# Two-layer decoder trunk: another order of the last down products at each stage end, and a weight split moved from unit 21 to unit 20

## The chip, the cores and the metric

One core of one Trainium2 chip runs the whole trunk in one launch. The metric is the device time of one execution in microseconds (us), the median of several runs.

## What is computed

x is 256 tokens by 1024 channels in float32. The trunk has two layers; each is a sandwich of feed-forward (FFN), mixer, FFN, and each of the six steps ends in a layer norm of the scaled residual:

```python
for i in range(DEPTH):
    x = post_norm(x, 0.5 * swiglu(x, w_gate[i, 0], w_up[i, 0], w_down[i, 0]), ln_g[i, 0], ln_b[i, 0])
    mix = pool_mixer(x, ...) if i % 2 == 0 else swa_sink_attention(x, ...)
    x = post_norm(x, mix, ln_g[i, 1], ln_b[i, 1])
    x = post_norm(x, 0.5 * swiglu(x, w_gate[i, 1], w_up[i, 1], w_down[i, 1]), ln_g[i, 2], ln_b[i, 2])
```

swiglu is silu(x Wg) * (x Wu), times Wd, with 2816 hidden channels. Layer 0 mixes by trailing means over 2, 4, 8 and 16 tokens and a linear map for each group of channels; layer 1 by windowed attention with 16 query heads, 4 key and value heads and sinks.

## The kernel before, in words

**Arithmetic.** Products run in a 32-bit matmul type on values that are split in two: `hi` is the value rounded to that type (a ScalarE copy), `lo` what is left (a VectorE subtraction). A product of two such values is three matmuls. Every weight is loaded raw by the SP queue, split by ScalarE (ACT, `*_hi`) and VectorE (DVE, `*_lo`), and some halves of the low part by GpSimd (POOL, `low_half`). `g_split` does a gate and up unit in two halves, `d_split` a down unit.

**Stages.** There are four FFN stages, f = 0 to 3, of 22 units of 128 hidden channels. For a unit, TensorE (PE) makes gate and up for all 256 tokens (`gate_up`), ACT and DVE make silu(gate) * up and its two parts, and PE multiplies by the down weights (`ffn_down`), adding into four PSUM banks ACC[t][h]: t is the token half (128 tokens), h the column half (512 of 1024 channels). One call for one t and one h is a group of three matmuls of 128x512 (lines 1226 to 1228, called by `down`); the last unit counts `acc_done` for each bank. Down of a unit runs a unit or more behind its gate and up.

**Stage end.** `last_u` is 18. Behind the gate and up of unit 21 PE issues, in this order: unit 19, t=0, h=1; unit 18, t=1, both h; units 20 and 21 of t=0, first h=0, then h=1; units 19 to 21 of t=1, first h=0, then h=1. The DVE norm (`layer_norm`, lines 942 to 973) takes t=0 and then t=1, each column half as its bank is counted: sum with the residual (L942), statistics (L948), centring (L960) and scaling (L973), with POOL's power for 1/sqrt. PE transposes the normed token half by column halves (`transposes`, L1328, four for each), ACT and DVE split it (L630, L989), and the next stage's first two units are done by token halves (`gate_up_tokens`, L1261 to L1266). Between stage 0 and stage 1 stands the pool mixer (`pool_pe`: `means` at L1043, `maps` at L1057); between stages 2 and 3 attention (`attention_pe`), whose output product `wo` uses the same `down`, k = 0 to 7, with k 5 to 7 of t=1 last by column halves.

**Order on the queues.** All order is written out by hand; each engine runs its instructions in program order, with waits on counting semaphores. `g_used` counts units whose gate and up are complete, so that their weight slots may be written; `d_used` the same for down slots; `g_hi_done`, `g_lo_done`, `h_hi_done`, `h_lo_done` count the parts. The first two units of the next stage are split at this stage's end: unit 0 at unit 20, and unit 1 at unit 21, where ACT does both halves of `hi` (line 599 and following), DVE the first half of `lo` (line 903 and following) and POOL the second. G0 is the number of units before a stage. The wait ahead of ACT's copies is

```python
if f is None:      # attention's q, k and v weights, behind stage 2
    after(act, g_used, G_QKV + (-1, 0, 0, 1, 3, 4)[u])
...
else:
    after(act, g_used, G0[f] + (-1, 0, 0, 2)[u] if u < 4 else G - 1 + 4 * it)
```

and the silu of a unit in `DIRECT` (0, 1 and 21) waits for `g_used >= G0[f] + u + 1`.

Of the kernel before, what the change touches and what calls it, by code (L numbers as in the profile page):

```python
# [27 lines left out]
UNITS = F // P  # L28
# [7 lines left out]
WINDOWS = (2, 4, 8, 16)  # L36
GC = D // len(WINDOWS)
# [7 lines left out]
POOL_UNITS = 2  # L45
# [24 lines left out]
def trunk_kernel(nc, x, positions, ln_g, ln_b, w_gate, w_up, w_down, pool_w, pool_b, pool_scale,  # L70
# [8 lines left out]
    with ExitStack() as ctx:  # L79
# [137 lines left out]
        def pool_raw(j):  # L217
            return raw_d[:, (D_POOL // 2) % 2, j, :]
# [30 lines left out]
        def next_first(f, u):  # L249
            return (f + 1 if f != 2 else None, u)  # L250
# [286 lines left out]
        def _(act):  # L537
# [42 lines left out]
            def unit(f, u, it=0):  # L580

                ahead = next_splits(f, u, it)
                if u not in DIRECT:
                    low_of(f, u, it)
                    for a in ahead[0:1]:
                        g_split(*a, halves=(0,))
                    silu_of(f, u, it)
                    for a in ahead[0:1]:
                        g_split(*a, halves=(1,))
                else:  # L590
                    silu_of(f, u, it)
                    for a in ahead[0:1]:
                        g_split(*a)
                h_hi_of(f, u, it)
                if f == 0 and u == 0:
                    g_split(0, RAW_UNITS)
                if u + 1 < UNITS:
                    d_split(D0[f] + u + 1, it)
                if f == 0 and u == UNITS - 2:
                    g_split(1, 0)  # L600
                if f < 3 and u == UNITS - 1:
                    g_split(*next_first(f, 1))

            def silu_tokens(f, t):
                act.wait_ge(*((tokens_done, f) if t == 0 else (g_used, G0[f] + 2)))
# [237 lines left out]
        def _(dve):  # L843
# [38 lines left out]
            def unit(f, u, it=0):  # L882

                ahead = next_splits(f, u, it)
                if u not in DIRECT:
                    gate_up_sum(f, u, it)
                    for a in ahead[0:1]:
                        g_split(*a, halves=(0,))
                    h_of(f, u, it)
                    for a in ahead[0:1]:  # L890
                        g_split(*a, halves=(1,))
                else:
                    h_of(f, u, it)
                    for a in ahead[0:1]:
                        g_split(*a)
                h_lo_of(f, u, it)
                if f == 0 and u == 0:
                    g_split(0, RAW_UNITS)
                if u + 1 < UNITS:
                    d_split(D0[f] + u + 1, it)  # L900
                if f == 0 and u == UNITS - 2:
                    g_split(1, 0, halves=(0,))
                if u == UNITS - 1:
                    if f == 0:
                        g_split(1, 0, halves=(1,))
                    elif f < 3:
                        g_split(*next_first(f, 1), halves=(0,))

            def h_tokens(f, t):
                dve.wait_ge(silu_done, UNITS * f + t + 1)  # L910
# [121 lines left out]
                else:  # L1032
                    layer_norm(5)

        def pool_pe(pe):

            def means(t, src, columns, first, last):

                for k in range(KT):
                    if k % 4 == 0 and t == src:  # L1040
                        pe.wait_ge(xn_done, 2 * t + k // 4 + 1)
                    out_ = ps[:, WORK + 2 * t + k // 4, (k % 4) * P:(k % 4 + 1) * P]
                    ins = pe.matmul(out_, xn[:, src, k * P:(k + 1) * P], band[:, k // 2, columns:columns + P],  # L1043
                                    start=first and k % 4 == 0, stop=last and k % 4 == 3)
                    if t == 0 and k == 0:
                        ins.then_inc(d_used, 1)
                    elif last and k % 4 == 3:
                        ins.then_inc(u_done, 1)

            def maps(t):  # L1050
                if t == 0:
                    pe.wait_ge(d_scaled, POOL_UNITS)
                for g in range(len(WINDOWS)):
                    if g % 2 == 0:
                        pe.wait_ge(u_sb, 2 * t + g // 2 + 1)
                    for j in range(2):
                        ins = pe.matmul(ACC[t][g // 2][:, (g % 2) * GC:(g % 2 + 1) * GC], uT[t][:, 2 * g + j, :],  # L1057
                                        pool_raw(j)[:, g * GC:(g + 1) * GC], start=j == 0, stop=j == 1)
                    if g % 2 == 1:
                        ins.then_inc(acc_done, 1)  # L1060

            pe.wait_ge(band_in, 16)
            pe.wait_ge(hf_done, UNITS)
            means(0, 0, 0, True, True)
            means(1, 0, P, True, False)
            maps(0)
            means(1, 1, S, False, True)
            maps(1)

        def attention_pe(pe, three, down, transposes):  # L1070

            ident = cst[:, 0, :]
            e = QKV_EVENT
# [91 lines left out]
                down(D_WO + k, xT_hi[:, k, :], xT_lo[:, k, :], ts, k == 0, k == WO_UNITS - 1, hs=hs)  # L1165

            transposes(e, 0)
            qkv(0, 0, 0, part=0, d_counted=True)
            qkv(0, 1, 0, part=0)
            qkv(0, 0, 0, part=1)  # L1170
# [43 lines left out]
                for k in (6, 7):  # L1214
                    wo(k, (0,), hs=(h,))
            for h in range(2):
                for k in range(5, 8):
                    wo(k, (1,), hs=(h,))


# [1 line left out]
        def _(pe):  # L1222
# [28 lines left out]
            def gate_up_tokens(f, t):  # L1251
# [6 lines left out]
                for k in range(KT):  # L1258
                    if k % 4 == 0:
                        pe.wait_ge(x_hi_done, 4 * e + 2 * t + k // 4 + 1)  # L1260
                    pe.matmul(out_, xT_hi[:, k, tok], w_hi[:, :, :, k, :], start=k == 0, stop=False)  # L1261
                    pe.matmul(out_, xT_hi[:, k, tok], w_lo[:, :, :, k, :], start=False, stop=False)  # L1262
                for k in range(KT):
                    if k % 4 == 0:
# [49 lines left out]
            def ffn_down(f, u, ts=(0, 1), it=0, hs=(0, 1)):  # L1314
# [5 lines left out]
                final = u == UNITS - 1  # L1320
                down(E, hT_hi[:, E % D_SLOTS, :], hT_lo[:, E % D_SLOTS, :], ts, u == 0, final, it, hs)

            def transposes(e, t, used=0):

                for q in range(2):
                    pe.wait_ge(*((xn_done, 4 * e + 2 * t + q + 1) if e > 0 else (x_in[t], 16)))
                    for k in range(4 * q, 4 * q + 4):
                        last = pe.transpose(x_bank(e, t, q)[:, (k % 4) * P:(k % 4 + 1) * P], xn[:, t, k * P:(k + 1) * P], ident)  # L1328
                        if k == 0 and used:
                            last.then_inc(d_used, used)  # L1330
                    last.then_inc(tr_done, 1)

            pe.wait_ge(ident_in, 16)
            for f in range(FFNS):
                e = FFN_EVENT[f]

                transposes(e, 0, used=(0, 2, 1, 1)[f])
                if f == 0:
                    gate_up_raw(0)
                    transposes(e, 1)  # L1340
# [24 lines left out]
                ffn_down(f, last_u + 1, (0,), hs=(0,))  # L1365
                gate_up(f, last_u + 3)
                ffn_down(f, last_u + 1, (0,), hs=(1,))
                ffn_down(f, last_u, (1,))
                for h in range(2):
                    for u in (last_u + 2, last_u + 3):  # L1370
                        ffn_down(f, u, (0,), hs=(h,))
                for h in range(2):
                    for u in range(last_u + 1, UNITS):
                        ffn_down(f, u, (1,), hs=(h,))
                if f == 0:
                    pool_pe(pe)
                if f == 2:
                    attention_pe(pe, three, down, transposes)

# [1 line left out]
_INS = ["x", "positions", "ln_g", "ln_b", "ffn_w_gate", "ffn_w_up", "ffn_w_down", "pool_w", "pool_b", "pool_scale",  # L1381
# [36 lines left out]
```

## Time and profile before

| | |
|---|---|
| median of 3 runs | 860.23 us (860.13 to 860.37) |
| profiled execution, its time | 860.7 us |
| its span | 858.9 us |
| PE busy | 841.1 us, 98% |
| DVE busy | 562.8 us, 66% |
| ACT busy | 419.3 us, 49% |
| POOL busy | 45.8 us, 5% |
| mean granted TensorE clock | 0.997 |

The span is the time from the first to the last instruction in the trace; the execution's own time has 1.8 us around it. The starts of matmuls are observed, their ends are modelled: a matmul of 128x512 is shown with some 0.4 us, but the next starts 0.23 us later, so neighbours overlap. Idle time in brackets is that of the engine just before the instruction, with what ended it.

### The profile page before, as it was taken

What the parts mean: (1) busy time and instruction counts of PE and PEld (TensorE: products, weight loads), DVE (VectorE), ACT (ScalarE), POOL (GpSimd) and SP (SyncE); (2) the same over time, 40 slices, a digit from 0 to 9 for tenths busy, and PEclk for the clock granted to TensorE, in tenths of its full rate; (3) what the DMA queues carried; (4) which work ended last, traced back from release to release, by engine and by line L of the source; (5) the groups of instructions that cost most, each with busy time, mean ns of one, the idle gap of its engine ahead of it and who ended that gap; (6) DMA issues with size and microseconds to landing.
All of it is one profiled execution on the core that took longest, in us unless ns stands there. A gap on an engine that the chain in (4) does not pass through costs nothing.

```text
span 858.9 us, 12145 instructions
## 1 busy us (share of the span) xinstructions
PE 841.1 (98%) x4484; PEld 711.5 (83%) x4484; DVE 562.8 (66%) x777; ACT 419.3 (49%) x651; POOL 45.8 (5%) x59
## 2 busy tenths in 40 slices
PE   7999999999999999999999999999999999999995
PEld 6888888888888888887888888887766888888885
DVE  2785655669846565668665565669898855655656
ACT  2554454552535455454445454554665544454540
POOL 0060000013000000002000000011001000000000
PEclk9999999999999999999999999999999999999998
DMA  9997555392755655556656556553454565465501
GB/s 277 348 325 243 177 195 178 116 294 101 250 192 180 203 188 195 172 179 228 205 158 229 168 177 206 185 196 123 167 167 154 172 224 196 154 229 168 182 1 49
DMA packets 116142, 162.17 MB, mean 189 GB/s; under 512 B 3936, under 2 KB 97632, under 8 KB 116112
## 3 DMA queue, kind: packets, MB, share of 16 engines
q1 hardware_dynamic: 112656, 152.06, 53.1%
q0 software_dynamic: 2496, 9.44, 3.3%
q8 instruction: 19, 0.31, 0.1%
q10 hardware_dynamic: 960, 0.27, 0.1%
q14 instruction: 11, 0.09, 0.0%
HBM read 160.70 MB, written 1.05 MB: 188 GB/s over the span
## 4 chain that ended last, share of the span: by engine, by line
PE 91%; DVE 4%; SPq 1%; DMA 1%; ACT 1%; issue 1%; POOL 0%; DVEq 0%; ACTq 0%
PE ps L1295 29%; PE ps L1293 17%; PE ps L1226 10%; PE ps L1227 10%; PE ps L1228 10%; PE ps L1292 4%; PE ps L1261 1%; DMA raw_g<-in_ffn_w_up 1%; PE ps L1262 1%; PE ps L1266 1%; PE ps L1092 1%; PE ps L1095 1%; PE ps L1101 1%; SPq L322 1%; PE ps L1328 1%; PE ps L1057 1%
## 5 line engine op out<-in xcount | busy, mean ns | idle before, releaser
L1295 PE MATMUL ps<-xT,g_hi 128*128 128x512 f32 x1064 | 379.3, 396 | 0.0
L1293 PE MATMUL ps<-xT,g_lo 128*128 128x256 f32 x1216 | 314.2, 279 | 0.0
L1293 PEld LDWEIGHTS ps<-xT,g_lo 128*128 128x128 f32 x1216 | 229.2, 188 | 12.5
L860 DVE TENSOR_TENSOR g_lo<-raw_g,g_hi 128x1024 fp32r<-128x1024 f32 x179 | 220.4, 1235 | 24.9 <-ACT g_hi L551 24.9
L1295 PEld LDWEIGHTS ps<-xT,g_hi 128*128 128x128 f32 x1064 | 199.7, 188 | 41.2
L870 DVE TENSOR_TENSOR gu<-ps,gu 128x512 f32<-128x512 f32 x76 | 52.5, 691 | 221.9 <-ACT gu L574 221.9
L551 ACT ACTIVATE g_hi<-raw_g 128x1024 fp32r<-128x1024 f32 x184 | 192.1, 1052 | 5.2 <-DMA raw_g<-in_ffn_w_up 3.6
L574 ACT ACTIVATE gu<-ps 128x512 f32<-128x512 f32 x76 | 45.6, 600 | 273.5 <-PE ps L1295 273.5
L1226 PE MATMUL ps<-d_hi,hT_hi 128*128 128x512 f32 x352 | 137.5, 391 | 0.0
L1227 PE MATMUL ps<-d_lo,hT_hi 128*128 128x512 f32 x352 | 137.0, 389 | 0.0
L1228 PE MATMUL ps<-d_hi,hT_lo 128*128 128x512 f32 x352 | 137.0, 389 | 0.0
L864 DVE TENSOR_TENSOR d_lo<-raw_d,d_hi 128x1024 fp32r<-128x1024 f32 x96 | 117.3, 1224 | 5.9 <-ACT d_hi L559 5.8
L559 ACT ACTIVATE d_hi<-raw_d 128x1024 fp32r<-128x1024 f32 x96 | 99.8, 1046 | 4.7 <-DMA raw_d<-in_ffn_w_down 4.7
L1228 PEld LDWEIGHTS ps<-d_hi,hT_lo 128*128 128x128 f32 x352 | 66.1, 188 | 14.2
L1227 PEld LDWEIGHTS ps<-d_lo,hT_hi 128*128 128x128 f32 x352 | 66.1, 188 | 14.0
L1226 PEld LDWEIGHTS ps<-d_hi,hT_hi 128*128 128x128 f32 x352 | 66.1, 188 | 10.6
L1292 PE MATMUL ps<-xT,g_hi 128*128 128x512 f32 x152 | 60.4, 397 | 1.0 <-DVE g_lo L860 1.0
L578 ACT ACTIVATE hT_hi<-hf_sink 128x256 fp32r<-128x256 f32 x82 | 34.3, 418 | 34.5 <-DVE hf_sink L875 34.2
L880 DVE TENSOR_TENSOR hT_lo<-hf_sink,hT_hi 128x256 fp32r<-128x256 f32 x82 | 34.4, 420 | 3.4 <-ACT hT_hi L578 3.4
L875 DVE TENSOR_TENSOR hf_sink<-gu 128x256 f32<-128x256 f32 x76 | 33.3, 438 | 1.0 <-ACT gu L568 1.0
L568 ACT ACTIVATE gu<-gu 128x256 f32<-128x256 f32 x76 | 30.9, 407 | 3.2 <-DVE gu L870 3.2
L1292 PEld LDWEIGHTS ps<-xT,g_hi 128*128 128x128 f32 x152 | 28.5, 188 | 4.3 <-DVE g_lo L860 1.5
(155 smaller groups left out, 662.0 us busy)
## 6 DMA issues: line engine op xcount, KB each, us to landing
raw_d<-in_ffn_w_down SPq DMA_DIRECT2D x87, 512.0 KB, 4.0
raw_g<-in_ffn_w_gate SPq DMA_DIRECT2D x43, 1024.0 KB, 5.5
raw_g<-in_ffn_w_up SPq DMA_DIRECT2D x43, 1024.0 KB, 7.9
raw_g<-in_attn_w_qkv SPq DMA_DIRECT2D x6, 1024.0 KB, 6.3
raw_d<-in_attn_w_o SPq DMA_DIRECT2D x8, 512.0 KB, 3.8
gb<-in_ln_g POOLq DMA_DIRECT2D x5, 512.0 KB, 3.9
gb<-in_ln_b POOLq DMA_DIRECT2D x4, 512.0 KB, 5.8
xn<-in_x SPq DMA_DIRECT2D x2, 512.0 KB, 6.1
```

The lines of the kernel that those rows point to most:

```text
L551: act.activation(g_half(g_hi, g_slot(f, u), half), src(G, half), ACT.Copy).then_inc(g_hi_done, 1)
L559: act.activation(d_hi[:, E % D_SLOTS, :], raw_d[:, (E // 2) % 2, E % 2, :], ACT.Copy).then_inc(d_hi_done, 1)
L574: act.activation(gu[:, u % 2, :, :], both[:, :, S:2 * S], ACT.Copy).then_inc(low_done, 1)
L860: dve.tensor_tensor(g_half(g_lo, g_slot(f, u), half), src(G, half), g_half(g_hi, g_slot(f, u), half).bitcast(f32), ALU.subtract).then_inc( ...
L864: dve.tensor_tensor(d_lo[:, E % D_SLOTS, :], raw_d[:, (E // 2) % 2, E % 2, :], d_hi[:, E % D_SLOTS, :].bitcast(f32), ALU.subtract).then_in ...
L870: dve.tensor_tensor(gu[:, u % 2, :, :], both[:, :, 0:S], gu[:, u % 2, :, :], ALU.add).then_inc(gu_done, 1)
L1226: pe.matmul(out_, l_hi, r_hi, start=start, stop=False)
L1227: pe.matmul(out_, l_hi, r_lo, start=False, stop=False)
L1228: return pe.matmul(out_, l_lo, r_hi, start=False, stop=stop)
L1292: pe.matmul(bank, w_hi, xT[:, k, :, :], start=True, stop=False)
L1293: last = pe.matmul(bank[:, S:2 * S], w_lo, xT_hi[:, k, :], start=False, stop=False)
L1295: last = pe.matmul(bank, w_hi, xT[:, k, :, :], start=False, stop=k == KT - 1)
```

## The change

Five edits, all in the order of work:

- At a stage's end the down products of t=0 come first (units 20 and 21, each with h=0 and h=1), and those of t=1 follow by columns: units 18 to 21 of h=0, then 18 to 20 of h=1.
- The very last group (unit 21, t=1, h=1) is `last_down`. In stage 0 it is issued behind the first `means` of the pool mixer, in stages 1 and 2 behind the transposes of t=0, in stage 3 at the end, where it was.
- In attention the group k=7, t=1, h=1 of `wo` stands behind the transposes of t=0 of stage 3.
- In the pool mixer the last of the four `maps` of t=1 stands behind the transposes of t=0 of stage 1.
- In stages 1 and 2 the first half of the next stage's unit 1 is split behind unit 20 (ACT and DVE); the second half on ACT stays behind unit 21.

The `d_used` increments move with the products; no instruction is added or removed.

```diff
--- before.py
+++ after.py
@@ -598,8 +598,10 @@
                     d_split(D0[f] + u + 1, it)
                 if f == 0 and u == UNITS - 2:
                     g_split(1, 0)
+                if f in (1, 2) and u == UNITS - 2:
+                    g_split(*next_first(f, 1), halves=(0,))
                 if f < 3 and u == UNITS - 1:
-                    g_split(*next_first(f, 1))
+                    g_split(*next_first(f, 1), halves=(0, 1)[f > 0:])
 
             def silu_tokens(f, t):
                 act.wait_ge(*((tokens_done, f) if t == 0 else (g_used, G0[f] + 2)))
@@ -900,11 +902,10 @@
                     d_split(D0[f] + u + 1, it)
                 if f == 0 and u == UNITS - 2:
                     g_split(1, 0, halves=(0,))
-                if u == UNITS - 1:
-                    if f == 0:
-                        g_split(1, 0, halves=(1,))
-                    elif f < 3:
-                        g_split(*next_first(f, 1), halves=(0,))
+                if f == 0 and u == UNITS - 1:
+                    g_split(1, 0, halves=(1,))
+                elif f in (1, 2) and u == UNITS - 2:
+                    g_split(*next_first(f, 1), halves=(0,))
 
             def h_tokens(f, t):
                 dve.wait_ge(silu_done, UNITS * f + t + 1)
@@ -1032,7 +1033,20 @@
                 else:
                     layer_norm(5)
 
-        def pool_pe(pe):
+        def pool_maps(pe, t, groups):
+
+            if t == 0:
+                pe.wait_ge(d_scaled, POOL_UNITS)
+            for g in groups:
+                if g % 2 == 0:
+                    pe.wait_ge(u_sb, 2 * t + g // 2 + 1)
+                for j in range(2):
+                    ins = pe.matmul(ACC[t][g // 2][:, (g % 2) * GC:(g % 2 + 1) * GC], uT[t][:, 2 * g + j, :],
+                                    pool_raw(j)[:, g * GC:(g + 1) * GC], start=j == 0, stop=j == 1)
+                if g % 2 == 1:
+                    ins.then_inc(acc_done, 1)
+
+        def pool_pe(pe, last_down):
 
             def means(t, src, columns, first, last):
 
@@ -1042,32 +1056,21 @@
                     out_ = ps[:, WORK + 2 * t + k // 4, (k % 4) * P:(k % 4 + 1) * P]
                     ins = pe.matmul(out_, xn[:, src, k * P:(k + 1) * P], band[:, k // 2, columns:columns + P],
                                     start=first and k % 4 == 0, stop=last and k % 4 == 3)
-                    if t == 0 and k == 0:
+                    if t == 1 and src == 0 and k == 0:
                         ins.then_inc(d_used, 1)
                     elif last and k % 4 == 3:
                         ins.then_inc(u_done, 1)
 
-            def maps(t):
-                if t == 0:
-                    pe.wait_ge(d_scaled, POOL_UNITS)
-                for g in range(len(WINDOWS)):
-                    if g % 2 == 0:
-                        pe.wait_ge(u_sb, 2 * t + g // 2 + 1)
-                    for j in range(2):
-                        ins = pe.matmul(ACC[t][g // 2][:, (g % 2) * GC:(g % 2 + 1) * GC], uT[t][:, 2 * g + j, :],
-                                        pool_raw(j)[:, g * GC:(g + 1) * GC], start=j == 0, stop=j == 1)
-                    if g % 2 == 1:
-                        ins.then_inc(acc_done, 1)
-
             pe.wait_ge(band_in, 16)
             pe.wait_ge(hf_done, UNITS)
             means(0, 0, 0, True, True)
+            last_down(0)
             means(1, 0, P, True, False)
-            maps(0)
+            pool_maps(pe, 0, range(4))
             means(1, 1, S, False, True)
-            maps(1)
-
-        def attention_pe(pe, three, down, transposes):
+            pool_maps(pe, 1, range(3))
+
+        def attention_pe(pe, three, down, transposes, last_down):
 
             ident = cst[:, 0, :]
             e = QKV_EVENT
@@ -1165,6 +1168,7 @@
                 down(D_WO + k, xT_hi[:, k, :], xT_lo[:, k, :], ts, k == 0, k == WO_UNITS - 1, hs=hs)
 
             transposes(e, 0)
+            last_down(2)
             qkv(0, 0, 0, part=0, d_counted=True)
             qkv(0, 1, 0, part=0)
             qkv(0, 0, 0, part=1)
@@ -1214,7 +1218,7 @@
                 for k in (6, 7):
                     wo(k, (0,), hs=(h,))
             for h in range(2):
-                for k in range(5, 8):
+                for k in range(5, 8 - h):
                     wo(k, (1,), hs=(h,))
 
 
@@ -1258,7 +1262,9 @@
                 for k in range(KT):
                     if k % 4 == 0:
                         pe.wait_ge(x_hi_done, 4 * e + 2 * t + k // 4 + 1)
-                    pe.matmul(out_, xT_hi[:, k, tok], w_hi[:, :, :, k, :], start=k == 0, stop=False)
+                    ins = pe.matmul(out_, xT_hi[:, k, tok], w_hi[:, :, :, k, :], start=k == 0, stop=False)
+                    if f > 1 and t == 0 and k == 0:
+                        ins.then_inc(d_used, 1)
                     pe.matmul(out_, xT_hi[:, k, tok], w_lo[:, :, :, k, :], start=False, stop=False)
                 for k in range(KT):
                     if k % 4 == 0:
@@ -1320,6 +1326,9 @@
                 final = u == UNITS - 1
                 down(E, hT_hi[:, E % D_SLOTS, :], hT_lo[:, E % D_SLOTS, :], ts, u == 0, final, it, hs)
 
+            def last_down(f):
+                ffn_down(f, UNITS - 1, (1,), hs=(1,))
+
             def transposes(e, t, used=0):
 
                 for q in range(2):
@@ -1334,7 +1343,13 @@
             for f in range(FFNS):
                 e = FFN_EVENT[f]
 
-                transposes(e, 0, used=(0, 2, 1, 1)[f])
+                transposes(e, 0, used=(0, 2, 0, 0)[f])
+                if f == 1:
+                    pool_maps(pe, 1, (3,))
+                elif f == 2:
+                    last_down(1)
+                elif f == 3:
+                    down(D_WO + 7, xT_hi[:, 7, :], xT_lo[:, 7, :], (1,), False, True, hs=(1,))
                 if f == 0:
                     gate_up_raw(0)
                     transposes(e, 1)
@@ -1365,17 +1380,18 @@
                 ffn_down(f, last_u + 1, (0,), hs=(0,))
                 gate_up(f, last_u + 3)
                 ffn_down(f, last_u + 1, (0,), hs=(1,))
-                ffn_down(f, last_u, (1,))
-                for h in range(2):
-                    for u in (last_u + 2, last_u + 3):
+                for u in (last_u + 2, last_u + 3):
+                    for h in range(2):
                         ffn_down(f, u, (0,), hs=(h,))
                 for h in range(2):
-                    for u in range(last_u + 1, UNITS):
+                    for u in range(last_u, UNITS - h):
                         ffn_down(f, u, (1,), hs=(h,))
                 if f == 0:
-                    pool_pe(pe)
+                    pool_pe(pe, last_down)
                 if f == 2:
-                    attention_pe(pe, three, down, transposes)
+                    attention_pe(pe, three, down, transposes, last_down)
+                if f == 3:
+                    last_down(f)
 
 # ---- launch: one core; inputs and outputs as the reference has them ----
 _INS = ["x", "positions", "ln_g", "ln_b", "ffn_w_gate", "ffn_w_up", "ffn_w_down", "pool_w", "pool_b", "pool_scale",
```

## Rows read from the trace of the kernel before

**Rows 1.** The page: span, and shares of the chain by engine

```profile
span 858.9 us, 12145 instructions
...
PE 91%; DVE 4%; SPq 1%; DMA 1%; ACT 1%; issue 1%; POOL 0%; DVEq 0%; ACTq 0%
```

**Rows 2.** Timeline, PE, end of second FFN: start us, us, engine, line, op, idle

```profile
387.38 0.40 PE L1226 MATMUL ps<-d_hi,hT_hi 128*128 128x512 f32 x1
...
390.58 0.39 PE L1228 MATMUL ps<-d_hi,hT_lo 128*128 128x512 f32 x1
...
396.02 0.39 PE L1228 MATMUL ps<-d_hi,hT_lo 128*128 128x512 f32 x1
396.26 1.32 PE L1328 MATMUL ps<-cst,xn 128*128 128x128 f32 x8
397.69 0.47 PE L1261 MATMUL ps<-g_hi,xT 128*128 128x512 f32 x1
398.00 0.39 PE L1262 MATMUL ps<-g_lo,xT 128*128 128x512 f32 x1
```

**Rows 3.** Timeline, ACT, the same end

```profile
387.57 0.38 ACT L568 ACTIVATE gu<-ps 128x256 f32<-128x256 f32 x1 [1.90 <-PE ps L1228]
388.45 0.42 ACT L578 ACTIVATE hT_hi<-hf_sink 128x256 fp32r<-128x256 f32 x1 [0.49 <-DVE hf_sink L875]
388.77 1.99 ACT L551 ACTIVATE g_hi<-raw_g 128x1024 fp32r<-128x1024 f32 x2
396.95 1.26 ACT L630 ACTIVATE xT<-ps 128x512 fp32r<-128x512 f32 x2 [6.19 <-PE ps L1328]
```

**Rows 4.** Timeline, DVE, the same end

```profile
387.99 0.42 DVE L875 TENSOR_TENSOR hf_sink<-gu,ps 128x256 f32<-128x256 f32 x1 [1.06 <-ACT gu L568]
388.90 0.42 DVE L880 TENSOR_TENSOR hT_lo<-hf_sink,hT_hi 128x256 fp32r<-128x256 f32 x1 [0.48 <-ACT hT_hi L578]
389.85 1.23 DVE L860 TENSOR_TENSOR g_lo<-raw_g,g_hi 128x1024 fp32r<-128x1024 f32 x1 [0.53 <-ACT g_hi L551]
391.00 0.69 DVE L942 SCALAR_TENSOR_TENSOR xn<-ps,xn 128x512 f32<-128x512 f32 x1
...
395.45 1.41 DVE L973 SCALAR_TENSOR_TENSOR xn<-xn,rstd,gb 128x512 f32<-128x512 f32 x2
396.78 0.69 DVE L942 SCALAR_TENSOR_TENSOR xn<-ps,xn 128x512 f32<-128x512 f32 x1
...
398.11 0.67 DVE L942 SCALAR_TENSOR_TENSOR xn<-ps,xn 128x512 f32<-128x512 f32 x1
```

**Rows 5.** Timeline, POOL, the same end

```profile
391.23 2.39 POOL L384 TENSOR_TENSOR g_lo<-raw_g,g_hi 128x1024 fp32r<-128x1024 f32 x1 [173.77 <-DVE g_lo L860]
```

**Rows 6.** Timeline, ACT, end of third FFN

```profile
573.75 0.38 ACT L568 ACTIVATE gu<-ps 128x256 f32<-128x256 f32 x1 [1.90 <-PE ps L1228]
```

**Rows 7.** Timeline, PE, first FFN's pool mixer into the second FFN

```profile
211.47 0.47 PE L1261 MATMUL ps<-g_hi,xT 128*128 128x512 f32 x1 [0.34 <-ACT xT L630]
```

**Rows 8.** Timeline, DVE, the same boundary

```profile
208.25 1.41 DVE L973 SCALAR_TENSOR_TENSOR xn<-xn,rstd,kx 128x512 f32<-128x512 f32 x2
```

**Rows 9.** Timeline, PE, end of attention

```profile
663.28 0.39 PE L1228 MATMUL ps<-d_hi,xT 128*128 128x512 f32 x1
663.78 1.32 PE L1328 MATMUL ps<-cst,xn 128*128 128x128 f32 x8
```

**Rows 10.** Timeline, DVE, end of attention

```profile
657.45 1.22 DVE L860 TENSOR_TENSOR g_lo<-raw_g,g_hi 128x1024 fp32r<-128x1024 f32 x1
658.58 0.68 DVE L942 SCALAR_TENSOR_TENSOR xn<-ps,xn 128x512 f32<-128x512 f32 x1
```

**Rows 11.** Timeline, DVE, end of kernel

```profile
844.82 0.69 DVE L942 SCALAR_TENSOR_TENSOR xn<-ps,xn 128x512 f32<-128x512 f32 x1 [1.68 <-PE ps L1228]
```

**Rows 12.** Timeline, PE, early stall of the first FFN

```profile
28.27 0.50 PE L1292 MATMUL ps<-xT,g_hi 128*128 128x512 f32 x1 [1.04 <-DVE g_lo L860]
```

**Rows 13.** Busy time in windows, stretch behind the last matmul: PE, PEld, DVE, ACT, POOL, clock, DMA

```profile
852.00:854.00 2.00, 0.00 (x0) 0.00 (x0) 1.90 (x6) 0.00 (x0) 0.17 (x1) 0.85 0.15 54
```

## The prediction

> **What bounds the kernel.** I read the chain of waits first: 91% of it is matrix work [rows 1], so only what makes TensorE (PE) stand still, or what follows its last product, can be won or lost. The change touches six such places: five where PE turns from one set of down products to a layer norm's result, and the end. Matmul ends are modelled, so I measure PE by starts. At the end of the second FFN the 39 down products start from 387.38 to 396.02, 0.227 us apart [rows 2]; a group of three (one unit, one token half, one column half) is 0.68. The transposes follow at once, because the norm of token half 0 has just delivered [rows 2, 4]. Its first column half ends at 396.20, its second at 396.86 (the two L973 take 1.41 from 395.45, 0.75 each with an overlap). So the second four transposes start at 396.9 and are through at about 397.4; the next product starts at 397.69 and its successor 0.31 later, not 0.23. That is 0.3 of gap plus 0.1 of restart which three independent products could fill.
>
> **A group less before the norm.** The new order finishes token half 0 one group sooner: behind the last gate and up product come four groups (unit 19's, unit 20's two, unit 21's first) instead of five before the norm's first column half is summed. At the kernel's end nothing is queued on DVE in between (it waited 1.68 us for PE) [rows 11], and all that follows is DVE's chain: **-0.68**. Unit 21's values are in time there: on the second FFN's times they are ready at 388.90 + 0.42 = 389.32 [rows 4], and three groups from 387.38 end at 389.44.
>
> **The split moved to unit 20, second and third FFN.** This is the largest term. ACT's `g_split` of the next stage's unit 1 waits (lines 545 and 549, the entry 0 for unit 1) for `g_used` to reach G0 of the next stage, which is the count that gate and up of unit 21 gives. Where it stands now, behind unit 21, that is long true. Behind unit 20 it is false until PE has ended unit 21, and ACT works in order: the silu of unit 21, which waits for the same count, is queued behind the copy. The row shows ACT idle 1.90 and released by PE at 387.57 [rows 3], the same in the third FFN at 573.75 [rows 6]. So the copy runs in that silu's place, not in the idle time.
> - ACT: copy from 387.57; it takes about 1.04 (the two from 388.77 take 1.99, and DVE starts on the first at 389.85) [rows 3, 4]; the silu follows at about 388.52.
> - DVE: its subtraction of that half is also put ahead of unit 21's product. It starts at 388.65; the next instruction comes 1.15 later (389.85 to 391.00) [rows 4], so the product that stood at 387.99 stands at 389.80, 1.81 later. The rounding and the rest keep their distances: unit 21 is ready at 389.32 + 1.81 = 391.13.
> - PE: unit 21 is wanted at 389.44, so PE stalls 1.7. The products of token half 1 are queued behind it. Restart as in [rows 2]: 0.1.
> - Norm of token half 0: DVE started it 0.42 after the third product's start (390.58, 391.00) [rows 2, 4]. Now the third product starts at about 391.73, the norm at 392.16: 1.16 later, though nothing else is queued ahead of it. First half ready at 397.36, second at 398.02.
> - PE's first group behind the stall ends at 391.95, and eight more (the other column half of unit 21, seven of token half 1) end at 397.4. So it meets the norm again, transposes from 397.4 and 398.07 to 398.5, then the three products with one restart (0.76). The successor of the first gate and up product starts at 399.5 instead of 398.00 [rows 2]: **+1.5** for each of the two ends.
> - ACT's copies of the transposes (released 0.7 after their start, 396.95) [rows 3] end before 399 and aren't late. POOL's subtraction of the other half, 2.39 [rows 5], waits for ACT's second copy, which moves from 389.7 to 390.6; it ends near 394.1, ahead of its next job and of its readers at 399. No transfer changes its issue order; the loads that wait for these splits have a whole stage before them.
> - Token half 1: DVE turns to it 1.16 later (396.78) [rows 4] and reads the last accumulator 1.33 after that (398.11) [rows 4], so at 399.27. The last product now ends behind the transposes, about 399.4. That is 0.15, less than the 0.35 by which PE has moved more than DVE.
>
> **End of attention.** DVE is the one that is late: its norm starts directly behind its own subtraction (657.45, 658.58) [rows 10], not on PE. PE's last product starts at 663.28 and the transposes wait until 663.78 [rows 9]. Taking one group away ahead of them only lengthens that idle time from 0.27 to 0.95; the group costs 0.76 behind the transposes, and fills the 0.4 that [rows 2] show there. **+0.35**.
>
> **Pool mixer.** The transposes are followed by an idle 0.34 and a restart [rows 7], and four mixer products (0.9) are moved into it. But the down group behind the first pooling products makes the norm of token half 1 wait, and the transposes then wait for DVE, whose second half ended at 209.66 [rows 8] and now comes some 0.35 later. Bounds: nothing lost to PE would be -0.4, all of DVE's delay kept would be +0.1; I take **-0.1**, near the DVE side because DVE has no gap in that stretch. Moved semaphore increments cost nothing: the slots that they release are wanted a unit or more later.
>
> **Sum.** -0.68 + 2 x 1.5 + 0.35 - 0.1 = +2.6 us. The profiled execution took 860.7 (span 858.9 and 1.8 around it) and would be 863.3; the median of the runs shown is 860.23, so **862.8**.
>
> **A rule beside a row.** When PE was last idle for good, the granted clock fell: between 852 and 854, with no product in it, it was 0.85 of 2.4 GHz, on its way to 1.2 [rows 13]. The longest stall behind a product that I cite, 1.04 in the first FFN, left the next one at 0.50 [rows 12], near the 0.47 of a restart behind the short gap and far from twice the 0.40 of a product [rows 2]; the new stalls are 1.7. I take no loss of clock. The Trainium skill ("TensorE: Matmul & The Clock Gate", Part 1) says that half rate is the default state and activity releases it, so that idleness gives it back; by that rule the two new stalls would each be a chance of a slow stretch. The trace agrees that idleness lowers the clock; that a stall of this length does, no row shows.
>
> **Rivals.**
> - *The wait is no wait* (0.1, the not-slower side). If the count were reached before ACT comes to the copy, ACT would do it in its 1.90 of idle [rows 3], DVE in its 1.06 [rows 4], and unit 21 would keep 389.32. The norm would start 0.68 earlier, PE would reach the transposes 0.68 earlier with it, and the three products would fill 0.4 and be out of the way of the norm: -0.4 per end. Sum -0.68 - 0.8 + 0.35 - 0.1 = -1.2, 859.0. It decides at whether that wait is passed before 387.5. Against it: the entry in the table is 0 and the silu's own count is the same number.
> - *Part of the delay is absorbed* (0.15). The stall is there, but half of it, if ACT's copy or DVE's subtraction overlaps more than their starts show, or attention's own waits swallow the third FFN's share. Third FFN's +1.5 gone or both halved: +1.1, 861.3.
> - *The last product holds up the second norm* (0.12). The accumulator of token half 1 comes behind the transposes; if DVE then delivers late to the next transposes, some 0.3 (a gap as that at 663.5 [rows 9]) is added at each of four boundaries: +3.8, 864.0.
> - *Clock falls after the stalls* (0.03). At 1.2 GHz the eight groups of 5.5 us behind each stall would take as much again: +11 and more, 874.
> - Forecast (0.6): 862.8.
>
> **Range and chances.** The bounds of the forecast's own terms (pool mixer -0.4 to +0.1, attention end 0 to +0.4, each FFN end 1.2 to 1.7) give 861.9 to 863.4. Down to 861.2 takes in the absorbed case, up to 864.2 the held second norm; outside are the no-wait case and the clock. A measurement here tells 0.2%, 1.7 us: below 858.5 is faster, above 861.95 slower. Faster 0.04, same 0.18 (no wait, absorbed, the low edge), slower 0.78.
>
> **What would show it.** In the changed kernel's trace: ACT's copy of 128x1024 directly at the end of unit 21's gate and up, with the silu behind it; a gap of 1.7 in PE before unit 21's first down product, in the second and third FFN and not in the first and fourth; DVE's norm at the kernel's end one group sooner after the last gate and up; three products between the transposes and the next gate and up; a longer gap ahead of the transposes at attention's end. I am wrong if the silu of unit 21 starts at its old distance from PE's last product, if PE's stall there is under 1, or if the time comes out below 860.2.

## The result, and the profile after

The changed kernel takes 862.91 us (median of 7 runs, 862.23 to 863.32) beside 860.23 for the kernel before (7 runs, 859.54 to 860.57). The ratio is 1.0031, with a 95% interval of 1.0020 to 1.0042: slower by some 0.3%. The forecast was 862.8, in a range of 861.2 to 864.2.

The page of the changed kernel, span and shares of the chain:

```profile
span 861.3 us, 12145 instructions
...
PE 92%; DVE 4%; ACT 1%; issue 1%; DMA 1%; POOL 0%; DVEq 0%; SPq 0%; ACTq 0%
```

The answers to [rows 1] hardly differ: as many instructions, and matrix work in 92% of the chain. A page of the whole doesn't show where 2.4 us of span came in; the timelines of the stage ends do. First ScalarE (ACT) at the end of the second FFN in the changed kernel, beside [rows 3]:

```profile
384.16 1.05 ACT L559 ACTIVATE d_hi<-raw_d 128x1024 fp32r<-128x1024 f32 x1
387.15 1.06 ACT L551 ACTIVATE g_hi<-raw_g 128x1024 fp32r<-128x1024 f32 x1 [1.95 <-PE ps L1232]
388.12 0.36 ACT L568 ACTIVATE gu<-ps 128x256 f32<-128x256 f32 x1
389.84 0.42 ACT L578 ACTIVATE hT_hi<-hf_sink 128x256 fp32r<-128x256 f32 x1 [1.35 <-DVE hf_sink L877]
```

ACT does unit 21's down weight (384.16), has nothing to do for 1.95 us, and then PE releases not the silu (L568) but the copy (L551). The silu follows 0.97 later. VectorE (DVE) in the same stretch, beside [rows 4]:

```profile
388.25 1.23 DVE L862 TENSOR_TENSOR g_lo<-raw_g,g_hi 128x1024 fp32r<-128x1024 f32 x1 [1.79 <-ACT g_hi L551]
389.39 0.41 DVE L877 TENSOR_TENSOR hf_sink<-gu,ps 128x256 f32<-128x256 f32 x1
390.29 0.43 DVE L882 TENSOR_TENSOR hT_lo<-hf_sink,hT_hi 128x256 fp32r<-128x256 f32 x1 [0.48 <-ACT hT_hi L578]
391.77 0.69 DVE L943 SCALAR_TENSOR_TENSOR xn<-ps,xn 128x512 f32<-128x512 f32 x1 [1.05 <-PE ps L1232]
```

The subtraction of the moved half (L862) waits 1.79 for ACT's copy, and unit 21's product (L877) stands behind it. L882 delivers unit 21, and the norm (L943) then waits 1.05 for PE, where before it followed DVE's own subtraction. What PE makes of that, beside [rows 2]:

```profile
386.89 0.40 PE L1230 MATMUL ps<-d_hi,hT_hi 128*128 128x512 f32 x1
...
388.74 0.39 PE L1232 MATMUL ps<-d_hi,hT_lo 128*128 128x512 f32 x1
390.77 0.50 PE L1230 MATMUL ps<-d_hi,hT_hi 128*128 128x512 f32 x1 [1.65 <-DVE hT_lo L882]
391.11 0.39 PE L1231 MATMUL ps<-d_lo,hT_hi 128*128 128x512 f32 x1
391.34 0.39 PE L1232 MATMUL ps<-d_hi,hT_lo 128*128 128x512 f32 x1
...
397.03 1.27 PE L1337 MATMUL ps<-cst,xn 128*128 128x128 f32 x8
398.06 0.47 PE L1230 MATMUL ps<-d_hi,hT_hi 128*128 128x512 f32 x1
...
398.83 0.40 PE L1265 MATMUL ps<-g_hi,xT 128*128 128x512 f32 x1
399.07 0.39 PE L1268 MATMUL ps<-g_lo,xT 128*128 128x512 f32 x1
```

The third group ends, 1.65 of idle time follow, unit 21 starts at 390.77, the transposes at 397.03, the last group at 398.06 and the first gate and up product at 398.83. The view of waits for PE has the same entry twice, 3.3 us in all:

```profile
PE ps L1230 <- DVE hT_lo L882: 3.3, 2, 1.6
```

And a window that begins in the first stall (columns as in [rows 13], the clock is third from the right) has the full clock, 1.00, as has 576 to 582 with the second stall:

```profile
390.00:396.00 6.00, 5.23 (x23) 4.34 (x24) 4.52 (x9) 1.21 (x2) 3.39 (x2) 1.00 0.30 91
```

At the end of attention the transposes wait for DVE, which [rows 9] showed as a gap of 0.27 between PE's own instructions:

```profile
659.31 0.50 PE L1230 MATMUL ps<-d_hi,xT 128*128 128x512 f32 x1
...
666.52 1.32 PE L1337 MATMUL ps<-cst,xn 128*128 128x128 f32 x8 [0.78 <-DVE xn L974]
...
668.61 0.39 PE L1268 MATMUL ps<-g_lo,xT 128*128 128x512 f32 x1
```

At the kernel's end DVE's norm, in [rows 11] at 844.82, is at 847.26, but the first down product there moved from 841.19 to 844.25, so it comes 3.0 behind it and not 3.6:

```profile
847.26 0.69 DVE L943 SCALAR_TENSOR_TENSOR xn<-ps,xn 128x512 f32<-128x512 f32 x1 [1.05 <-PE ps L1232]
```

To compare kernels I use distances in the timelines of one profiled execution each: from the first down product behind unit 21's gate and up to the second of the next gate and up (or q, k and v) products, and at the kernel's end to the end of the span; at attention's end from the first of the output products behind the last values. Most of them repeat within 0.03, all within 0.1, between kernels that are equal in that place, where the intervals of the times are some 0.8 us to either side.

| distance, us | FFN 1 with mixer | FFN 2 | FFN 3 | attention | end |
|---|---|---|---|---|---|
| before | 23.05 | 10.62 | 10.57 | 8.95 | 17.71 |
| changed | 22.95 | 12.18 | 12.17 | 9.30 | 17.05 |
| difference | -0.10 | +1.56 | +1.60 | +0.35 | -0.66 |
| forecast | -0.1 | +1.5 | +1.5 | +0.35 | -0.68 |

The differences add up to +2.75; the medians are 2.68 apart. The two profiled spans are only 2.4 apart because the first of these distances begins at 188.72 before and at 188.37 in the changed kernel, behind a stretch that the change doesn't touch.

### The profile page after: what moved, and what is told of

Read it like the earlier page. It is cut to its first block, busy times and chain, and to the rows that moved or that the text cites. A ratio compares the mean times of both kernels' runs of the same rounds, so it can differ in the third digit from the quotient of the medians.

```text
span 861.3 us, 12145 instructions
## 1 busy us (share of the span) xinstructions
PE 841.9 (98%) x4484; PEld 712.5 (83%) x4484; DVE 563.2 (65%) x777; ACT 419.9 (49%) x651; POOL 45.9 (5%) x59
## 3 DMA queue, kind: packets, MB, share of 16 engines
HBM read 160.70 MB, written 1.05 MB: 188 GB/s over the span
## 4 chain that ended last, share of the span: by engine, by line
PE 92%; DVE 4%; ACT 1%; issue 1%; DMA 1%; POOL 0%; DVEq 0%; SPq 0%; ACTq 0%
PE ps L1301 29%; PE ps L1299 16%; PE ps L1230 10%; PE ps L1232 10%; PE ps L1231 10%; PE ps L1298 4%; PE ps L1265 1%; PE ps L1268 1%; PE ps L1272 1%; PE ps L1250 1%; PE ps L1095 1%; PE ps L1098 1%; PE ps L1104 1%; PE ps L1337 1%; PE ps L1044 1%
## 5 line engine op out<-in xcount | busy, mean ns | idle before, releaser
L862 DVE TENSOR_TENSOR g_lo<-raw_g,g_hi 128x1024 fp32r<-128x1024 f32 x179 | 220.5, 1236 | 26.6 <-ACT g_hi L551 26.6
L1301 PEld LDWEIGHTS ps<-xT,g_hi 128*128 128x128 f32 x1064 | 199.7, 188 | 41.2
L551 ACT ACTIVATE g_hi<-raw_g 128x1024 fp32r<-128x1024 f32 x184 | 192.5, 1053 | 8.4 <-PE ps L1232 3.9
L882 DVE TENSOR_TENSOR hT_lo<-hf_sink,hT_hi 128x256 fp32r<-128x256 f32 x82 | 34.5, 420 | 3.4 <-ACT hT_hi L578 3.4
L877 DVE TENSOR_TENSOR hf_sink<-gu 128x256 f32<-128x256 f32 x76 | 33.3, 438 | 1.0 <-ACT gu L568 1.0
L568 ACT ACTIVATE gu<-gu 128x256 f32<-128x256 f32 x76 | 31.0, 408 | 3.2 <-DVE gu L872 3.2
L384 POOL TENSOR_TENSOR g_lo<-raw_g,g_hi 128x1024 fp32r<-128x1024 f32 x5 | 12.0, 2402 | 372.9 <-ACT g_hi L551 346.4
```

The costliest lines, as they stand in the source:

```text
L551: act.activation(g_half(g_hi, g_slot(f, u), half), src(G, half), ACT.Copy).then_inc(g_hi_done, 1)
L862: dve.tensor_tensor(g_half(g_lo, g_slot(f, u), half), src(G, half), g_half(g_hi, g_slot(f, u), half).bitcast(f32), ALU.subtract).then_inc( ...
L1301: last = pe.matmul(bank, w_hi, xT[:, k, :, :], start=False, stop=k == KT - 1)
```

## Experiments on the stall

**The wait one lower.** The slot that the moved copy writes is free long before: only the first units of a stage read it. So the count that it waits for can be one lower, the end of unit 20. All else as changed.

```diff
-                        after(act, g_used, G_QKV + (-1, 0, 0, 1, 3, 4)[u])
+                        after(act, g_used, G_QKV + (-1, -1, 0, 1, 3, 4)[u])
-                        after(act, g_used, G0[f] + (-1, 0, 0, 2)[u] if u < 4 else G - 1 + 4 * it)
+                        after(act, g_used, G0[f] + (-1, 0 if f == 3 else -1, 0, 2)[u] if u < 4 else G - 1 + 4 * it)
```

> The changed kernel, but ACT's copy of the next stage's unit 1 waits for a g_used one lower (unit 20 ended), which its slot allows. My theory (ACT's wait in front of unit 21's silu makes the stall): ACT copies in its idle time before unit 21's gate and up have ended, PE's stall of 1.65 us before unit 21's down product is gone in both places, the norm of token half 0 starts 0.7 earlier against the first down product than in the kernel before, and each of the two ends takes 0.4 less than before instead of 1.6 more: 859.0 us, 3.9 below the changed kernel. Rival (DVE's subtraction queued in front of unit 21's product is enough for the stall): the stall stays near 0.9 and the time near 861.

Measured: 858.67 us beside 859.91 of the kernel before on the same chip, ratio 0.9986 (0.9977 to 0.9995). ACT, second FFN:

```profile
383.50 1.05 ACT L559 ACTIVATE d_hi<-raw_d 128x1024 fp32r<-128x1024 f32 x1
384.46 1.04 ACT L551 ACTIVATE g_hi<-raw_g 128x1024 fp32r<-128x1024 f32 x1
386.44 0.38 ACT L568 ACTIVATE gu<-ps 128x256 f32<-128x256 f32 x1 [0.94 <-PE ps L1232]
```

The copy follows the down weight's at once, and the silu stands directly at PE's release, with 0.94 of idle time left. DVE:

```profile
385.73 1.22 DVE L862 TENSOR_TENSOR g_lo<-raw_g,g_hi 128x1024 fp32r<-128x1024 f32 x1
386.86 0.42 DVE L877 TENSOR_TENSOR hf_sink<-gu,ps 128x256 f32<-128x256 f32 x1
...
389.25 0.69 DVE L943 SCALAR_TENSOR_TENSOR xn<-ps,xn 128x512 f32<-128x512 f32 x1 [1.06 <-PE ps L1232]
```

Unit 21's product follows the subtraction without a wait, and the norm starts 3.0 behind the first down product (386.24) instead of 3.6. PE has no wait for unit 21 at either end. The distances are 10.30 and 10.30: 0.32 and 0.27 less than before, where 0.4 was expected, and 1.9 less than changed. One less in the wait, at each of the two ends, is thus worth some 3.8 us of the kernel. The rival is out: DVE's subtraction is still ahead of unit 21's product and costs nothing.

**The split back behind unit 21.** Both edits of `unit` undone, the new order of products kept:

```diff
-                if f in (1, 2) and u == UNITS - 2:
-                    g_split(*next_first(f, 1), halves=(0,))
-                if f < 3 and u == UNITS - 1:
-                    g_split(*next_first(f, 1), halves=(0, 1)[f > 0:])
+                if f < 3 and u == UNITS - 1:
+                    g_split(*next_first(f, 1))
```

and on DVE as before the change.

> The changed order of products with the split of unit 1 back behind unit 21, on ACT and DVE. My theory: no stall, but DVE's subtraction then holds the norm at its old start (3.6 us after the first down product), so the group taken away ahead of the transposes only turns into idle time and costs 0.35 behind them at each of the two ends; with attention's end +0.35, the mixer -0.15 and the kernel's end -0.66 it makes +0.25: 860.5. Rival (the order of products alone is worth its 0.7 at each end): 859.0 or less.

Measured: 860.11 beside 859.91, ratio 1.0001 (0.9992 to 1.0010); distances 10.90 and 10.91, +0.28 and +0.34. The norm starts at 3.62 as before the change. PE at the second FFN's end:

```profile
395.70 1.32 PE L1336 MATMUL ps<-cst,xn 128*128 128x128 f32 x8 [0.37 <-DVE xn L973]
```

PE is now at the transposes too early and waits there. So the order of products needs the moved split: without it DVE is still busy when the first accumulator is complete, and a group taken away ahead of the transposes comes back behind them.

**The split alone.** The kernel before with only the two edits of `unit`.

```diff
-                if f < 3 and u == UNITS - 1:
-                    g_split(*next_first(f, 1))
+                if f in (1, 2) and u == UNITS - 2:
+                    g_split(*next_first(f, 1), halves=(0,))
+                if f < 3 and u == UNITS - 1:
+                    g_split(*next_first(f, 1), halves=(0, 1)[f > 0:])
```

> The kernel before with only the split moved to unit 20. My theory: unit 21's values come 1.8 us later; in the old order PE wants them one group later, so it stalls 1.0 instead of 1.65; the norm starts 1.15 later, and each of the two ends takes 1.15 more: 862.5. Rival (the loss comes from the new order of products): as before, 860.2.

Measured: 862.41 beside 859.91, ratio 1.0028 (1.0017 to 1.0039); distances 11.89 and 11.82, +1.27 and +1.25. PE:

```profile
390.35 0.50 PE L1227 MATMUL ps<-d_hi,hT_hi 128*128 128x512 f32 x1 [0.96 <-DVE hT_lo L882]
```

The stall is there without the new order, shorter by the one group that PE still has to do. The loss belongs to the split with its wait. The moved split with the lower wait in the old order of products was not run.

**DVE's half back, ACT's not.** To share the 1.8 us between the two engines:

```diff
-                if f == 0 and u == UNITS - 1:
-                    g_split(1, 0, halves=(1,))
-                elif f in (1, 2) and u == UNITS - 2:
-                    g_split(*next_first(f, 1), halves=(0,))
+                if u == UNITS - 1:
+                    if f == 0:
+                        g_split(1, 0, halves=(1,))
+                    elif f < 3:
+                        g_split(*next_first(f, 1), halves=(0,))
```

> The changed kernel with DVE's subtraction of that half back behind unit 21, ACT's copy where the change put it. My theory splits the 1.8 us between them: ACT's copy delays unit 21 by 0.95, DVE's subtraction by the rest. Here the stall is 0.85, the norm starts 0.3 later than before, each end takes 0.7 more than before: 861.2. Rival (ACT's copy alone carries the whole delay): the stall stays at 1.65 and the time at 862.9.

Measured: 860.63 beside 859.91, ratio 1.0010 (1.0000 to 1.0019); distances 11.32 and 11.31, +0.70 and +0.74. DVE, second FFN, and then PE:

```profile
387.81 0.42 DVE L877 TENSOR_TENSOR hf_sink<-gu,ps 128x256 f32<-128x256 f32 x1 [2.06 <-ACT gu L568]
...
390.21 0.69 DVE L944 SCALAR_TENSOR_TENSOR xn<-ps,xn 128x512 f32<-128x512 f32 x1
```

```profile
389.20 0.50 PE L1231 MATMUL ps<-d_hi,hT_hi 128*128 128x512 f32 x1 [0.78 <-DVE hT_lo L882]
```

With ACT's copy alone in the way the product comes 1.62 behind the first down product (386.19), with DVE's as well 2.50 (389.39 behind 386.89), before 0.61. So ACT's copy costs 1.0 and DVE's subtraction 0.9 more, but the second only because the first has made it late; with the lower wait it cost nothing. The stall is 0.78 instead of 1.65.

## Experiments on the other ends

**Attention's end alone**, the kernel before with only its last output group behind the transposes:

```diff
                 for h in range(2):
-                for k in range(5, 8):
+                for k in range(5, 8 - h):
                     wo(k, (1,), hs=(h,))
...
+                if f == 3:
+                    down(D_WO + 7, xT_hi[:, 7, :], xT_lo[:, 7, :], (1,), False, True, hs=(1,))
```

> The kernel before with only the last attention output group moved behind the transposes. My theory: the transposes stay where DVE puts them, PE's wait ahead of them grows from 0.27 to 0.95, and the next gate and up comes 0.35 later; 860.3 us. Rival (it fills the gap and is worth up to 0.4): 859.5.

Measured: distance 9.30, +0.35; 860.10 beside 859.95, ratio 1.0002 (0.9993 to 1.0012), which can't tell 0.35 us. PE, the first six of the eight transposes:

```profile
663.15 1.10 PE L1328 MATMUL ps<-cst,xn 128*128 128x128 f32 x6 [0.79 <-DVE xn L973]
```

They start 7.21 behind the first output product (655.94), exactly as before: DVE sets them.

**The kernel's end alone**, the new order in the fourth FFN only (`if f < 3:` the old order, `else:` the new).

> The kernel before with the new order of down products in the fourth FFN alone. My theory: DVE's chain behind the last gate and up is the end of the kernel and starts one group earlier: 0.66 less from the first down product to the end, 859.3 us. Rival (PE's own end is what counts): nothing.

Measured: distance 17.07, -0.64; 859.52 beside 859.95, ratio 0.9994 (0.9985 to 1.0003). The distance shows the gain; the times agree in size but don't resolve it.

**The lower wait, and attention's end undone.** This is the changed kernel less its two losses.

> The changed kernel with the lower wait, and attention's output products all ahead of the transposes again, as before the change. My theory (DVE is late there, so a group behind the transposes only costs): the way from the last attention products to the next gate and up is 0.35 shorter than in the kernel with the lower wait alone; 858.3 us. Rival (the group behind the transposes fills idle time there too): no shorter, 858.7 or more.

Measured: 858.30 beside 859.95, ratio 0.9981 (0.9972 to 0.9990). Attention's end is back at 8.95, the FFN ends stay at 10.30.

**POOL takes both halves** of the fourth FFN's unit 1, on top of that:

```diff
+                low_half(3, 1, 0)
                 low_half(3, 1, 1)
...
             o_lo(len(TASKS) - 1)
-            g_split(3, 1, halves=(0,))
```

> As the kernel with attention's end undone, and besides POOL subtracts both halves of the fourth FFN's unit 1, so that DVE's subtraction no longer stands in front of the norm at attention's end. My theory: the norm then starts on its accumulator instead of on DVE, 0.3 earlier, and PE meets the transposes with hardly any wait: 858.0. Rival (POOL's second subtraction, 2.4 us behind the first, ends too late for the power that the norm needs, or for the next gate and up): no gain or a loss up to 1.

Measured: 858.61 beside 859.95, ratio 0.9982 (0.9973 to 0.9991), not to be told from the one before it; the gain of 0.3 that was expected isn't seen. The norm does start 0.32 earlier (1.69 behind the first output product, before 2.01), but the distance shrinks by 0.12 only. POOL:

```profile
655.95 4.94 POOL L384 TENSOR_TENSOR g_lo<-raw_g,g_hi 128x1024 fp32r<-128x1024 f32 x2 [15.95 <-DVE g_lo L862]
660.85 1.02 POOL L451 TENSOR_TENSOR rstd<-rstd,mhalf 128x1 f32<-128x1 f32 x1
```

The two subtractions end at 660.89, and the power that the norm waits for (L451) stands behind them, though its input was complete at 660.64 (DVE's instruction at 660.49 takes 0.15). DVE's scaling starts 1.47 behind its centring (662.03 and 660.56), where it is 1.32 in the kernel without this edit (661.23 and 659.91). So the rival's mechanism is real and took 0.15 of the 0.32; the rest of what is missing went in small steps of DVE's ahead of that.

**The mixer.** In the changed kernel DVE waits there for the group that was put behind the first pooling products:

```profile
199.44 0.69 DVE L943 SCALAR_TENSOR_TENSOR xn<-ps,xn 128x512 f32<-128x512 f32 x1 [0.91 <-PE ps L1232]
```

That is the second column half of token half 1. The scaling that the transposes need comes later by it, 19.89 behind the first down product where it was 19.53 before [rows 8]:

```profile
208.26 1.41 DVE L974 SCALAR_TENSOR_TENSOR xn<-xn,rstd,kx 128x512 f32<-128x512 f32 x2
```

With the group ahead of the first `means` again:

```diff
-            means(0, 0, 0, True, True)
             last_down(0)
+            means(0, 0, 0, True, True)
```

> As the kernel with the lower wait and attention's end undone; besides, in the first FFN's end the last down group stands ahead of the first pooling products instead of behind them. My theory (that group made DVE wait 0.9 us for the accumulator of token half 1, and this ate the 0.4 that moving four mixer products behind the transposes would give): DVE's wait goes, the transposes of the second FFN are PE's to start, at 20.5 us after the first down product instead of 20.8, and the next gate and up comes 0.45 earlier: 857.85 us. Rival (the mixer's end gains nothing by the order): as that kernel, 858.3.

Measured: 857.78 beside 859.80, ratio 0.9977 (0.9967 to 0.9986); distance 22.38, 0.55 less than the 22.93 of the kernel that it builds on. PE:

```profile
208.72 1.04 PE L1337 MATMUL ps<-cst,xn 128*128 128x128 f32 x8
...
210.69 0.39 PE L1268 MATMUL ps<-g_lo,xT 128*128 128x512 f32 x1
```

The eight transposes run without a pause (1.04 from the start of the first to the end of the last, 1.23 for the changed kernel's), and from the first of them to the second gate and up product it is 1.97, where it was 1.68 before the change: the four products behind the transposes, 0.9 of work, cost 0.3 there.

**The last group between the transposes**, second and third FFN, on top of that: `last_down` moves from behind `transposes(e, 0)` to behind its first four.

> As the kernel before it in this call, and at the ends of the second and third FFN the last down group stands between the two sets of four transposes instead of behind both. My theory: it fills the 0.2 us in which the second four wait for DVE, less a second restart of 0.08 behind the first four: 0.1 less at each of the two ends, 857.65 us. Rival (the copies of the second four then come too late for the gate and up products): 0.3 more at each, 858.4.

Measured: 857.48 beside 859.80, ratio 0.9974 (0.9964 to 0.9984); distances 10.09 and 10.08, 0.22 less each instead of 0.1. PE, second FFN:

```profile
393.95 0.61 PE L1336 MATMUL ps<-cst,xn 128*128 128x128 f32 x4
394.32 0.48 PE L1229 MATMUL ps<-d_hi,hT_hi 128*128 128x512 f32 x1
394.63 0.39 PE L1230 MATMUL ps<-d_lo,hT_hi 128*128 128x512 f32 x1
...
395.10 0.60 PE L1336 MATMUL ps<-cst,xn 128*128 128x128 f32 x4
395.45 0.48 PE L1264 MATMUL ps<-g_hi,xT 128*128 128x512 f32 x1
395.77 0.39 PE L1267 MATMUL ps<-g_lo,xT 128*128 128x512 f32 x1
```

Behind the first four transposes the group starts at once, and the second four follow it without waiting for DVE. The second gate and up product comes 1.82 after the first transpose, 2.04 with the group behind all eight. The next products don't wait for the copies, so that rival is out. This is the fastest version: 0.26% below the kernel before and, by the two ratios, 0.57% below the changed one (0.9974 over 1.0031; the two were not timed on one chip).

## Why the prediction was right

- *The split moved to unit 20* (+1.5 each, measured +1.56 and +1.60): every step is in the rows. The copy stands in the silu's place, and DVE's subtraction behind it and in front of the product. The 1.7 of the forecast is counted by starts; by starts the stall is 1.80 (the third group would have been followed at 388.97, unit 21 starts at 390.77), and the 1.65 in brackets is the same stall counted from a modelled end. The norm is 1.26 later (4.88 against 3.62 behind the first down product) and not 1.16: the copy starts 0.26 behind that product where the silu started 0.19, it releases DVE 1.10 behind its start and not 1.08, and PE starts 0.05 behind the end of DVE's last subtraction (390.72). The forecast had PE start without that 0.05, but its time for the third product, 391.73, is 0.05 more than its own steps give (391.13 and two starts of 0.227 with a restart of 0.1 make 391.68). The lower wait shows that it is the wait, the split alone that it isn't the order of products, and DVE's half back how the delay is shared.
- *A group less before the norm* (-0.68, measured -0.66 at the end of the kernel): as worked out, and the same 0.6 shows at each FFN's norm once the stall is gone.
- *End of attention* (+0.35, measured +0.35 in the change and again alone): DVE was late, so the time ahead of the transposes only changed hands.
- *Pool mixer* (-0.1, measured -0.10): the size was picked between bounds 0.5 apart, so that it fits to 0.01 is luck. Its reason holds: DVE's scaling comes 0.36 later where 0.35 was said, and the transposes start at 20.78 where they start at 20.41 with the group ahead of the pooling products (21.37 before the change). The lower bound doesn't hold: with that wait gone the end is 0.67 shorter than before (22.38 against 23.05), and the prediction took -0.4 as the most that could be won.
- *The wait is no wait* fell with the first timeline. Its price was too high: without the stall an FFN's end gains 0.3, not 0.4.
- *Part absorbed* fell too: from the third FFN's first down product to attention's first output product it is 83.02 before and 84.59 changed, so its 1.6 passes through attention whole.
- *The second norm held up*: DVE does wait for the late accumulators, but no such wait reached PE: the next eight transposes start 1.56 later behind the first down product (17.42 against 15.86), as much as the end of the second FFN has lost already. It cost something only in the mixer, where the group came ahead of a long stretch of DVE's own.
- *Clock*: full in the window behind the stall, and the second product of the stalled group comes 0.34 behind the first, the third 0.23 behind that. The part of the forecast that took no loss of clock stands. The rule of the Trainium skill ("TensorE: Matmul & The Clock Gate", Part 1) is neither shown nor refuted for the new stalls: these traces say only that two stalls of 1.65 us, each inside a dense run of products, left the clock at 1.00.

That the total was so near (862.8, measured 862.91) is partly luck. The five terms make +2.57 and the distances +2.75, with the errors of 0.06, 0.10 and 0.02 all on one side; the mixer's term could as well have been picked a few tenths off; and the interval of the ratio is 0.9 us to either side, so the times can't confirm a forecast to 0.1.

## What to carry to other kernels

When an instruction is moved to an earlier place in an in-order queue, its wait must be read again: a count that was long reached in the old place may be the very one that the next instruction waits for, and then the moved work runs in front of it instead of in the idle time. Before taking work away ahead of a hand-over, ask who is late there: where the consumer's input is bound by the other engine, what is moved behind it wins nothing ahead of it, and behind it costs what the idle time there doesn't hold (here 0.35 of 0.76). And a new order of work pays off only if the engine that must use it is free by then: at the ends of the second and third FFN it cost 0.3 while DVE was kept by a subtraction, and won 0.3 once that had moved with the right wait.

## What was not expected of the hardware

The gain of 0.2 from putting three matmuls between two sets of four transposes was twice what was expected from a wait of 0.2 and a restart of 0.08. Eight transposes in one go, with that wait between them, keep the next product 1.03 behind the first of them (394.51 to 395.54 in the kernel with the group ahead of the pooling products); the two sets of four keep it 0.37 and 0.35. So 0.3 was to be had, and not 0.2. Behind the first four, which had no wait, the restart was 0.31 to the second product (394.32 to 394.63), and behind the second four the next product came 0.35 after their start. The first matmul behind the transposes keeps its successor back by 0.08 there, with no wait in sight, and that behind the stall of the changed kernel by 0.11 (390.77 to 391.11). POOL's subtraction of 128x1024 takes 2.4 [rows 5] where DVE's takes 1.2 [rows 4], and two of them in a row took 4.94 where POOL did both halves.
